# Two quarters of a split-precision feed-forward: high and low part of h in one pass of 512 columns, up and down chunks alternating

## The chip, the cores and the metric

The kernel runs on one core of a Trainium2 chip. The metric is the device time of one execution in microseconds.

## The reference

Two blocks run one after the other on 256 tokens of width 1024. The first has two layers, each with three kinds of attention and then a feed-forward; the second mixes attention, a Fourier, a convolution and a pooling branch and is untouched here. All is in float32. The feed-forward of the first block is

```
hdn = modulate(rmsnorm(x, norm2_g[l]), shift2, scale2)
ff = jnp.square(jax.nn.relu(hdn @ w_ff1[l])) @ w_ff2[l]
x = x + gate2[:, None, :] * ff
```

with `w_ff1` 1024 x 4096 and `w_ff2` 4096 x 1024.

## The kernel before

A float32 product is made of three products of rounded parts: each weight chunk is split into `w_hi` and `w_lo`, each activation into a high and a low part, and hi\*hi, hi\*lo and lo\*hi are added up in PSUM. A chunk is 8 x 128 rows by 256 columns of weights (1 MB). For each of the 8 row tiles and each of two halves of 128 output features, TensorE (PE) does three matmuls of 128x256 (lines 1758, 1760, 1762 in `products`), 48 in a chunk.

The program of a layer is a list of chunks, `j` = 0 to 74; the last 32, from `FF` = 43 on, are the feed-forward. I call `j - FF` the step, 0 to 31. The 4096 hidden features are in four quarters; `FF_ORDER` says that the steps are up 0, up 1, down 0, up 2, down 1, up 3, down 2, down 3, four chunks of each. An up chunk writes one of the two PSUM banks `dense` in turn; a down chunk adds to one of four banks `acc` (`first_s` twice, `first_t`, `first_o`).

Every engine walks the same list. Around step `j` each does, in this order:

- ScalarE (ACT): rounds the first half of chunk `j + 2` to `w_hi` (line 554; it waits until the PE has used the first half of chunk `j`), evacuates chunk `j`, rounds the second half of chunk `j + 2`. To evacuate an up chunk is ReLU (2140) and twice a square (2145, 2149).
- VectorE (DVE): makes `w_lo` of the first half of chunk `j + 2` by subtraction (560), makes the low part of the squared activation (2379), makes `w_lo` of the second half, and then does the *folds* of that step.

A fold belongs to other work: a 1 MB unit of a modulation matrix is multiplied by a column and added to the unit before (lines 588 and 592 in layer 0, 608 and 610, in two visits, in layer 1). The table `FOLDS` puts them at these steps of the feed-forward: in layer 0 one each at 2, 3 and 5, two at 7, one each at 8 to 26; in layer 1 one visit each at 3 to 10 and 13 to 20. When a group of folds is complete, the PE adds it up over the partitions in `group_sum` (line 245), placed in its queue at a fixed step. In layer 0 the sum at step 12 waits for the fold of step 10, that at 20 for the fold of step 18; in layer 1 the sum at step 12 waits for the fold of step 10, that at 22 for the fold of step 20. At step 4 of either layer another sum of the same line stands, over a unit that is not folded. `keep_group` (569, 574) moves such sums off on the DVE.

SyncE (SP) issues the loads in one queue: weight chunk `j` when the DVE has finished `w_lo` of chunk `j - 3`, and between them the fold units, each when an earlier fold is done.

```
for j in range(N_CHUNKS):
...
    split_ahead(partial(split_low, dve), base + j, 0)
...
    evacuate(j)
    split_ahead(partial(split_low, dve), base + j, 1)
...
    if j >= FF:
        for unit in folds_at(base + j):
            fold(dve, unit)
```

Of the kernel before, what the change touches and what calls it, by code (L numbers as in the profile page):

```python
# [51 lines left out]
GB, WSB, GC, WMB, GA, WMLA, WOUT, FF = 21, 25, 27, 31, 33, 37, 39, 43  # L52
FF_ORDER = [("up", 0), ("up", 1), ("down", 0), ("up", 2), ("down", 1), ("up", 3), ("down", 2), ("down", 3)]
FF_STEPS = [(kind, q, c) for kind, q in FF_ORDER for c in range(4)]
N_CHUNKS = FF + len(FF_STEPS)

# [81 lines left out]


def out_first(j):  # L140
    return WSB if j < GC else WMB if j < GA else WMLA
# [7 lines left out]
def units_of(j):  # L149

    if is_down(j):
        return 0
    if j == UKV:
        return 4
    return 2 if is_out(j) else 1

# [4 lines left out]
DONE = [sum(max(1, units_of(i % N_CHUNKS)) for i in range(g)) for g in range(DEPTH * N_CHUNKS + 1)]  # L161
UP_NO = {FF + i: 4 * q + c for i, (kind, q, c) in enumerate(FF_STEPS) if kind == "up"}
DOWN_END = {q: FF + i + 1 for i, (kind, q, c) in enumerate(FF_STEPS) if kind == "down" and c == 3}

# [11 lines left out]
def constants_first():  # L176
# [34 lines left out]
                    prob_ready=24, arg_ready=8, arg_exp=8, prob_t_ready=24, o_hi_made=12, o_ready=12,  # L211
                    gate_ready=12, merge_added=8, merged_hi=4, merged_ready=4, ff_hi_made=16, ff_ready=16,
                    x_ready=4)
# [64 lines left out]
def layers(nc, a, keep, out):  # L278
    with ExitStack() as stack:
# [1444 lines left out]
        def layer(l, next_x_ready, following=None):  # L1724
# [14 lines left out]
                Counted(first_sems[n], FIRST_COUNTS[n] * l) for n in ("gate_ready", "merge_added", "merged_hi", "merged_ready"))  # L1739
            ff_hi_made, ff_ready, x_ready = (Counted(first_sems[n], FIRST_COUNTS[n] * l) for n in ("ff_hi_made", "ff_ready", "x_ready"))  # L1740

# [4 lines left out]
            def tensor(pe):  # L1746
# [172 lines left out]
                def by_features(j, out, w, x, nk, width=P, **options):  # L1919
# [3 lines left out]
                    return products(j, outs, nk, **options)  # L1923

                def lead(j, chunks):

# [23 lines left out]
                def chunk(j):  # L1950
# [31 lines left out]
                    elif is_out(j):  # L1982
                        branch = {WSB: SB, WMB: MB, WMLA: MLA}[out_first(j)]
                        reach(pe, o_ready, 4 * branch + 4)
                        for e in range(2):
                            by_features(j, two(bank_of(u + e)), [part[:, :, CW * e:CW * e + CW] for part in w],
                                        (o_hi[branch], o_lo[branch]), 4, frees=e == 1).then_inc(unit_done, 1)
                    elif is_down(j):
                        _, q, c = FF_STEPS[j - FF]
# [46 lines left out]
            def scalar(act, link, logged):  # L2036
# [54 lines left out]
                def after_values(n):  # L2091
                    act.wait_ge(values_done[l], n + 1)
                    act.activation(o_hi[n // 4][:, n % 4, :], o_bank[:, 0:S], ACT.Copy).then_inc(o_hi_made.sem, 1)

                def evacuate(j):
                    if UQ <= j < UKV or is_out(j) or WOUT <= j < FF or is_down(j):
                        return
                    for e in range(units_of(j)):
# [39 lines left out]
                        else:  # L2138
                            n, (_, q, c) = UP_NO[j], FF_STEPS[j - FF]
                            act.activation(relu[n % 2], two, ACT.Relu).then_inc(done, 1)  # L2140
                            wait_evacuated(act, u)
                            if n >= 2:

                                reach(act, ff_ready, n - 1)
                            act.activation(relu_sq[n % 2], relu[n % 2], ACT.Square)
                            if c == 0 and q >= 2:

                                act.wait_ge(unit_done, DONE[base + DOWN_END[q - 2]])
                            act.activation(ff_hi[q % 2][:, 2 * c:2 * c + 2, :], relu[n % 2],
                                           ACT.Square).then_inc(ff_hi_made.sem, 1)  # L2150

# [85 lines left out]
            def vector(dve, link):  # L2237
# [111 lines left out]
                def evacuate_out(j, e):  # L2349
# [10 lines left out]
                    if first == 2:  # L2360
                        wait_evacuated(dve, u)
                        dve.tensor_tensor(merged[:, t:t + 2, :], merged[:, t:t + 2, :], gated[:, t:t + 2, :],
                                          ALU.add).then_inc(merge_added.sem, 1)

                def evacuate(j):
                    if QL <= j < CKV:
# [3 lines left out]
                    if j in ropes:  # L2370
                        rope(j)
                    elif WOUT <= j < FF:
                        u = RING[base + j]
                        dve.wait_ge(unit_done, DONE[base + j] + 1)
                        residual(2 * (j - WOUT), dense[u % 2], 16, j == FF - 1).then_inc(evacuated[u % 2], 1)
                    elif j in UP_NO:
                        n, (_, q, c) = UP_NO[j], FF_STEPS[j - FF]
                        reach(dve, ff_hi_made, n + 1)
                        dve.tensor_tensor(ff_lo[q % 2][:, 2 * c:2 * c + 2, :], relu_sq[n % 2],
                                          ff_hi[q % 2][:, 2 * c:2 * c + 2, :].bitcast(F32),  # L2380
                                          ALU.subtract).then_inc(ff_ready.sem, 1)
# [437 lines left out]
```

## Time and profile before

| | |
|---|---|
| time, median of 3 runs | 1375.18 us (1375.07 to 1375.34) |
| the profiled execution | 1374.65 us, its span 1372.5 us |
| PE busy in the span | 1329.8 us, 97% |
| DVE busy | 942.5 us, 69% |
| ACT busy | 737.4 us, 54% |
| feed-forward of layer 0, layer 1 | from 337 to 526 us, from 831 to about 1026 us |

The profiled execution lasted 2.15 us longer than its span, the part that lies around the recorded instructions. Matmuls overlap in the records: the distance from start to start says what one costs.

### The profile page before, as it was taken

How to read it: one execution, taken by the hardware profiler on the slowest of the kernel's cores; microseconds unless marked ns; L12 is line 12 of the kernel's file. 1: busy time of each engine (PE TensorE's matmuls, PEld its weight loads, DVE VectorE, ACT ScalarE, POOL GpSimd, SP SyncE). 2: the span in 40 equal slices, each digit the busy share in tenths (PEclk: the TensorE clock that was granted, in tenths of full speed). 3: DMA queues.
4: the chain of work that ended last, by engine and by line, in shares of the span. 5: the costliest groups of instructions: out<-in, count | busy, mean ns of one | idle time of the engine just before them, and what ended most of it. 6: DMA issues, size and time to landing. Idle time of an engine off the chain costs nothing.

```text
span 1372.5 us, 24612 instructions
## 1 busy us (share of the span) xinstructions
PE 1329.8 (97%) x10268; PEld 1218.2 (89%) x10268; DVE 942.5 (69%) x1367; ACT 737.4 (54%) x1203; POOL 60.5 (4%) x49
## 2 busy tenths in 40 slices
PE   6999999999999999999999999999999999998998
PEld 3998899998999998998999998999997778687987
DVE  3877976667688876478755566978575656538673
ACT  3565475564645534555666555544554555426562
POOL 0010000201000001010000210000100000011000
PEclk9999999999999999999999999999999999999999
DMA  9974555677799995744744467976552122132430
GB/s 345 356 237 166 168 209 180 211 255 240 234 323 374 357 372 181 228 132 132 275 154 128 150 218 261 318 244 220 177 167 92 62 93 81 43 101 73 144 123 31
DMA packets 194721, 269.51 MB, mean 196 GB/s; under 512 B 5037, under 2 KB 174386, under 8 KB 188338
## 3 DMA queue, kind: packets, MB, share of 16 engines
q1 hardware_dynamic: 194610, 267.94, 57.8%
q8 instruction: 81, 1.33, 0.4%
q14 instruction: 30, 0.25, 0.1%
HBM read 266.87 MB, written 1.05 MB: 195 GB/s over the span
## 4 chain that ended last, share of the span: by engine, by line
PE 78%; DVE 12%; ACT 5%; issue 3%; SPq 1%; DMA 1%; DVEq 0%; ACTq 0%
PE first_dense L1758 13%; PE first_dense L1762 12%; PE first_dense L1760 12%; PE first_dense L1075 5%; PE first_dense L1078 5%; PE first_dense L1077 5%; DVE first_w_lo L560 3%; PE first_s L1758 2%; PE first_s L1762 2%; PE first_s L1760 2%; PE first_dense L1937 2%; ACT first_w_hi L554 1%; PE first_o L1762 1%; PE first_t L1762 1%; PE first_t L1760 1%
## 5 line engine op out<-in xcount | busy, mean ns | idle before, releaser
L560 DVE TENSOR_TENSOR first_w_lo<-first_raw,first_w_hi 128x1024 fp32r<-128x1024 f32 (+2 forms) x304 | 366.5, 1219 | 185.0 <-ACT first_w_hi L554 182.9
L554 ACT ACTIVATE first_w_hi<-first_raw 128x1024 fp32r<-128x1024 f32 (+2 forms) x304 | 313.5, 1041 | 232.2 <-PE first_dense L1762 90.6
L1758 PE MATMUL first_dense<-first_h_parts,first_w_hi 128*128 128x256 f32 x1312 | 374.5, 285 | 3.0 <-DVE first_h_parts L2392 1.7
L1760 PE MATMUL first_dense<-first_h_parts,first_w_hi 128*128 128x256 f32 x1312 | 371.1, 283 | 0.0
L1762 PE MATMUL first_dense<-first_h_parts,first_w_lo 128*128 128x256 f32 x1312 | 371.0, 283 | 0.0
L1758 PEld LDWEIGHTS first_dense<-first_h_parts,first_w_hi 128*128 128x128 f32 x1312 | 251.5, 192 | 12.4 <-issue 8.1
L1760 PEld LDWEIGHTS first_dense<-first_h_parts,first_w_hi 128*128 128x128 f32 x1312 | 251.6, 192 | 0.0
L1762 PEld LDWEIGHTS first_dense<-first_h_parts,first_w_lo 128*128 128x128 f32 x1312 | 251.6, 192 | 0.0
L1077 PE MATMUL first_dense<-first_parts,first_w_hi 128*128 128x512 f32 (+1 forms) x400 | 137.0, 342 | 0.0
L1075 PE MATMUL first_dense<-first_h_parts,first_w_hi 128*128 128x512 f32 (+1 forms) x336 | 118.4, 352 | 1.4 <-DVE first_w_lo L731 0.9
L1078 PE MATMUL first_dense<-first_h_parts,first_w_lo 128*128 128x512 f32 (+1 forms) x336 | 115.6, 344 | 0.0
L731 DVE TENSOR_TENSOR first_w_lo<-first_raw,first_w_hi 128x1024 fp32r<-128x1024 f32 x56 | 68.1, 1224 | 48.2 <-ACT first_w_hi L724 47.8
L724 ACT ACTIVATE first_w_hi<-first_raw 128x1024 fp32r<-128x1024 f32 x56 | 58.9, 1055 | 48.7 <-PE first_dense L1078 48.6
L1077 PEld LDWEIGHTS first_dense<-first_parts,first_w_hi 128*128 128x128 f32 x400 | 75.8, 190 | 9.4 <-issue 1.0
L1758 PE MATMUL first_dense<-first_parts,first_w_hi 128*128 128x256 f32 x280 | 80.3, 287 | 0.7 <-DVE first_area L2291 0.7
L1760 PE MATMUL first_dense<-first_parts,first_w_hi 128*128 128x256 f32 x280 | 79.2, 283 | 0.0
L1762 PE MATMUL first_dense<-first_parts,first_w_lo 128*128 128x256 f32 x280 | 79.2, 283 | 0.0
L1075 PEld LDWEIGHTS first_dense<-first_h_parts,first_w_hi 128*128 128x128 f32 x336 | 63.6, 189 | 16.7 <-issue 8.7
L1758 PE MATMUL first_s<-first_parts,first_w_hi 128*128 128x256 f32 x256 | 72.8, 284 | 0.0
L1762 PE MATMUL first_s<-first_parts,first_w_lo 128*128 128x256 f32 x256 | 72.4, 283 | 0.0
L1760 PE MATMUL first_s<-first_parts,first_w_hi 128*128 128x256 f32 x256 | 72.4, 283 | 0.0
L1078 PEld LDWEIGHTS first_dense<-first_h_parts,first_w_lo 128*128 128x128 f32 x336 | 63.6, 189 | 7.7
(418 smaller groups left out, 2624.4 us busy)
## 6 DMA issues: line engine op xcount, KB each, us to landing
first_raw<-in_w_in SPq DMA_DIRECT2D x78, 1024.0 KB, 5.3
first_raw<-in_w_ff SPq DMA_DIRECT2D x64, 1024.0 KB, 7.9
first_units<-in_w_ada SPq DMA_DIRECT2D x34, 1024.0 KB, 6.6
first_units<-in_w_mod SPq DMA_DIRECT2D x17, 1024.0 KB, 6.8
first_raw<-in_w_out SPq DMA_DIRECT2D x16, 1024.0 KB, 5.3
first_mb<-in_w_ada SPq DMA_DIRECT2D x10, 1024.0 KB, 7.9
first_mb<-in_w_mod SPq DMA_DIRECT2D x7, 1024.0 KB, 7.3
first_raw<-in_w_uq SPq DMA_DIRECT2D x6, 768.0 KB, 4.4
```

The source lines that it names most:

```text
L554: act.activation(w_hi[g % SPLIT][:, c], raw[g % CHUNK_RING][:, c], ACT.Copy).then_inc(hi_made, 1)
L560: dve.tensor_tensor(w_lo[g % SPLIT][:, c], raw[g % CHUNK_RING][:, c], w_hi[g % SPLIT][:, c].bitcast(F32), ALU.subtract).then_inc(lo_made, 1)
L724: act.activation(in_tiles(w_hi[place2(l, c, SPLIT)][:])[:, r, :], in_tiles(raw[place2(l, c, CHUNK_RING)][:])[:, r, :], ACT.Copy).then_inc( ...
L731: engine.tensor_tensor(in_tiles(w_lo[place2(l, c, SPLIT)][:])[:, r, :], in_tiles(raw[place2(l, c, CHUNK_RING)][:])[:, r, :], hi.bitcast(F3 ...
L1075: pe.matmul(out, still[0](t), moving[0](t), start=t == i == 0, stop=False, skip_group_check=True)
L1077: pe.matmul(out, still[0](t), moving[1](t), start=False, stop=False, skip_group_check=True)
L1078: last = pe.matmul(out, still[1](t), moving[0](t), start=False, stop=t == KT - 1, skip_group_check=True)
L1758: pe.matmul(out, still[0](t), moving[0](t), start=start and t == n == 0, stop=False, skip_group_check=True)
L1760: pe.matmul(out, still[0](t), moving[1](t), start=False, stop=False, skip_group_check=True)
L1762: last = pe.matmul(out, still[1](t), moving[0](t), start=False, stop=stop and t == nk - 1, skip_group_check=True)
L1937: pe.matmul(at[i][:, c, :], part[:, t, c * P:(c + 1) * P], h_hi[:, t, :], start=part is w[i][0] and t == c == 0, stop=False, skip_group_ch ...
```

## The change

The up chunks of quarters 1 and 2 (`is_wide`, the second and third of four) take both `dense` banks. For each row tile and half of the features there is one matmul of `w_hi` against high and low part of h side by side, 512 columns (line 1941 of the new file), whose two halves land in the two halves of a bank, and one of `w_lo` against the high part, 256 columns (1943). ACT copies the right half of each bank out (`part_moved`), the DVE adds the left half to it, and then ACT does the ReLU and the two squares from SBUF as before. The low part of the square is made by the DVE at the next step, a down chunk. The order of the steps becomes up 0 (0 to 3), then up 1 and down 0 in turn (4 to 11), up 2 and down 1 in turn (12 to 19), and up 3, down 2, down 3 as before (20 to 31). The tables of folds and sums are unchanged, and so are their step numbers.

```
+FF_ORDER = [[("up", 0)], [("up", 1), ("down", 0)], [("up", 2), ("down", 1)], [("up", 3)], [("down", 2)], [("down", 3)]]
+FF_STEPS = [(kind, q, c) for kinds in FF_ORDER for c in range(4) for kind, q in kinds]
+def is_wide(j):
+    return j >= FF and FF_STEPS[j - FF][0:2] in (("up", 1), ("up", 2))
...
-    return 2 if is_out(j) else 1
+    return 2 if is_out(j) or is_wide(j) else 1
...
+                def wide_up(j):
+                    w = [view(part[(base + j) % SPLIT], j) for part in (w_hi, w_lo)]
+                    banks = [bank_of(RING[base + j] + c) for c in range(2)]
+                    for t in range(KT):
+                        if 2 * t in (0, KT):
+                            pe.wait_ge(lo_made, 2 * (base + j) + 1 + (t > 0))
+                        for c in range(2):
+                            f = slice(c * P, (c + 1) * P)
+                            pe.matmul(two(banks[c]), w[0][:, t, f], h_parts[:, :, t, :], start=t == 0, stop=False,
+                                      skip_group_check=True)
+                            last = pe.matmul(banks[c][:, 0:S], w[1][:, t, f], h_hi[:, t, :], start=False,
+                                             stop=t == KT - 1, skip_group_check=True)
+                            if t == KT - 1:
+                                last.then_inc(unit_done, 1)
+                        if 2 * t + 2 == KT:
+                            last.then_inc(half_used, 1)
...
# ACT
+                    if is_wide(j):
+                        r, u = relu[UP_NO[j] % 2], RING[base + j]
+                        for e in range(2):
+                            act.wait_ge(unit_done, DONE[base + j] + e + 1)
+                            act.activation(r[:, e, :], dense[(u + e) % 2][:, S:2 * S], ACT.Copy).then_inc(part_moved.sem, 1)
+                        for e in range(2):
+                            wait_evacuated(act, u + e)
+                        link(act.activation(r, r, ACT.Relu))
+                        up_squares(j)
+                        return
...
# DVE
+                    elif is_wide(j):
+                        r, u = relu[UP_NO[j] % 2], RING[base + j]
+                        for e in range(2):
+                            reach(dve, part_moved, 2 * WIDE_NO[j] + e + 1)
+                            dve.tensor_tensor(r[:, e, :], r[:, e, :], dense[(u + e) % 2][:, 0:S],
+                                              ALU.add).then_inc(evacuated[(u + e) % 2], 1)
                     elif j in UP_NO:
+                        up_low(j)
+                    elif is_down(j) and is_wide(j - 1):
+                        up_low(j - 1)
```

On the DVE, layer 0, steps 14 and 15 before (both up 2): for each, `w_lo` of the first half, the low part of the square, `w_lo` of the second half, a fold.

```order
L560 TENSOR_TENSOR first_w_lo<-first_raw,first_w_hi 128x1024 [waits first_hi_made]
L2379 TENSOR_TENSOR first_parts<-first_gate,first_parts 128x512 [waits first_ff_hi_made]
L560 TENSOR_TENSOR first_w_lo<-first_raw,first_w_hi 128x1024 [waits first_hi_made]
L592 SCALAR_TENSOR_TENSOR first_units<-first_units,first_small 128x2048 [waits first_unit_folded,first_raw_in3]
L560 TENSOR_TENSOR first_w_lo<-first_raw,first_w_hi 128x1024 [waits first_hi_made]
L2379 TENSOR_TENSOR first_parts<-first_gate,first_parts 128x512 [waits first_ff_hi_made]
L560 TENSOR_TENSOR first_w_lo<-first_raw,first_w_hi 128x1024 [waits first_hi_made]
L592 SCALAR_TENSOR_TENSOR first_mb<-first_mb,first_small,first_units 128x2048 [waits first_unit_folded,first_raw_in5]
```

The same two steps after the change (an up chunk of quarter 2, then a down chunk of quarter 1).

```order
L566 TENSOR_TENSOR first_w_lo<-first_raw,first_w_hi 128x1024 [waits first_hi_made]
L2428 TENSOR_TENSOR first_gate<-first_gate,first_dense 128x256 [waits first_part_moved] x2
L566 TENSOR_TENSOR first_w_lo<-first_raw,first_w_hi 128x1024 [waits first_hi_made]
L598 SCALAR_TENSOR_TENSOR first_units<-first_units,first_small 128x2048 [waits first_unit_folded,first_raw_in3]
L566 TENSOR_TENSOR first_w_lo<-first_raw,first_w_hi 128x1024 [waits first_hi_made]
L2409 TENSOR_TENSOR first_parts<-first_gate,first_parts 128x512 [waits first_ff_hi_made]
L566 TENSOR_TENSOR first_w_lo<-first_raw,first_w_hi 128x1024 [waits first_hi_made]
L598 SCALAR_TENSOR_TENSOR first_mb<-first_mb,first_small,first_units 128x2048 [waits first_unit_folded,first_raw_in5]
```

Two additions stand now between the two subtractions of the up step, and the low part has gone to the step behind; every fold has kept its place behind the second subtraction.

On ACT, an up step before:

```order
L554 ACTIVATE first_w_hi<-first_raw 128x1024 [waits first_half_used,first_raw_in2]
L2140 ACTIVATE first_gate<-first_dense 128x512 [waits first_unit_done]
L2145 ACTIVATE first_gate<-first_gate 128x512 [waits first_ff_ready,first_evacuated0]
L2149 ACTIVATE first_parts<-first_gate 128x512
L554 ACTIVATE first_w_hi<-first_raw 128x1024 [waits first_unit_done,first_raw_in2]
```

and an up step of quarter 1 after:

```order
L560 ACTIVATE first_w_hi<-first_raw 128x1024 [waits first_half_used,first_raw_in1]
L2140 ACTIVATE first_gate<-first_dense 128x256 [waits first_unit_done] x2
L2143 ACTIVATE first_gate<-first_gate 128x512 [waits first_evacuated1,first_evacuated0]
L2127 ACTIVATE first_gate<-first_gate 128x512 [waits first_ff_ready,first_act_link]
L2130 ACTIVATE first_parts<-first_gate 128x512
L560 ACTIVATE first_w_hi<-first_raw 128x1024 [waits first_unit_done,first_raw_in1]
```

The ReLU now stands behind a wait for the DVE's two additions, and the second rounding still stands behind the ReLU and the squares.

On the PE, the sum at step 12 of layer 0 before, between a down chunk and an up chunk:

```order
L1762 MATMUL first_o<-first_parts,first_w_lo0 128x256
L245 MATMUL first_misc<-first_units,keep_consts 32x512 [waits first_ssq_used,first_group_kept,first_unit_folded]
L245 MATMUL first_misc<-first_units,keep_consts 32x512 x3
L1758 MATMUL first_dense0<-first_h_parts,first_w_hi1 128x256 [waits first_lo_made,first_evacuated0]
L1760 MATMUL first_dense0<-first_h_parts,first_w_hi1 128x256
```

and after:

```order
L1769 MATMUL first_o<-first_parts,first_w_lo0 128x256
L251 MATMUL first_misc<-first_units,keep_consts 32x512 [waits first_ssq_used,first_group_kept,first_unit_folded]
L251 MATMUL first_misc<-first_units,keep_consts 32x512 x3
L1941 MATMUL first_dense0<-first_h_parts,first_w_hi1 128x512 [waits first_lo_made,first_evacuated1,first_evacuated0]
L1943 MATMUL first_dense0<-first_h_parts,first_w_lo1 128x256
```

The sum with its wait for the folds has kept its place; the up chunk behind it waits for both banks.

## Rows read from the trace of the kernel before

**Rows 1.** The page: busy time, share of the span and instructions of each engine.

```profile
PE 1329.8 (97%) x10268; PEld 1218.2 (89%) x10268; DVE 942.5 (69%) x1367; ACT 737.4 (54%) x1203; POOL 60.5 (4%) x49
```

**Rows 2.** Windows: stretch and length, busy time by engine, clock, DMA share, GB/s.

```profile
408.40:454.50 46.10, 46.10 (x388) 46.10 (x384) 39.72 (x31) 23.97 (x29) 0.00 (x0) 1.00 1.05 375
855.70:901.70 46.00, 46.00 (x387) 46.00 (x384) 41.25 (x40) 24.06 (x30) 0.00 (x0) 1.00 0.93 319
```

**Rows 3.** Timeline of the PE, layer 0, step 12: start, us, engine, line, tiles, count.

```profile
407.18 0.28 PE L1762 MATMUL first_o<-first_parts,first_w_lo 128*128 128x256 f32 x1
407.39 1.06 PE L245 MATMUL first_misc<-first_units,keep_consts 128*32 128x512 f32 x8
408.39 0.38 PE L1758 MATMUL first_dense<-first_h_parts,first_w_hi 128*128 128x256 f32 x1
```

**Rows 4.** Timeline of the PE: matmuls of 512 columns and 256 columns.

```profile
1100.08 0.39 PE L1075 MATMUL first_dense<-first_h_parts,first_w_hi 128*128 128x512 f32 x1
1100.31 0.39 PE L1077 MATMUL first_dense<-first_parts,first_w_hi 128*128 128x512 f32 x1
...
407.06 0.28 PE L1760 MATMUL first_o<-first_parts,first_w_hi 128*128 128x256 f32 x1
```

**Rows 5.** Timeline of the PE: the other three sums of groups of folds.

```profile
454.65 1.06 PE L245 MATMUL first_misc<-first_mb,keep_consts 128*32 128x512 f32 x8
...
901.93 1.07 PE L245 MATMUL first_misc<-first_pair_sums,first_choose 128*32 128x256 f32 x16
...
961.62 1.07 PE L245 MATMUL first_misc<-first_pair_sums,first_choose 128*32 128x256 f32 x16 [0.84 <-DVE first_pair_sums L610]
```

**Rows 6.** Timeline of the DVE, layer 0, steps 4 and 5, 10, and 14.

```profile
366.40 1.22 DVE L560 TENSOR_TENSOR first_w_lo<-first_raw,first_w_hi 128x1024 fp32r<-128x1024 f32 x1
...
371.09 0.44 DVE L569 STREAM_TRANSPOSE first_small<-first_misc 128x256 f32<-128x256 f32 x1
...
371.73 1.22 DVE L560 TENSOR_TENSOR first_w_lo<-first_raw,first_w_hi 128x1024 fp32r<-128x1024 f32 x1
...
404.98 2.35 DVE L592 SCALAR_TENSOR_TENSOR first_units<-first_units,first_small,first_mb 128x2048 f32<-128x2048 f32 x1
...
428.11 0.68 DVE L2379 TENSOR_TENSOR first_parts<-first_gate,first_parts 128x512 fp32r<-128x512 f32 x1
428.73 1.23 DVE L560 TENSOR_TENSOR first_w_lo<-first_raw,first_w_hi 128x1024 fp32r<-128x1024 f32 x1
429.87 2.35 DVE L592 SCALAR_TENSOR_TENSOR first_units<-first_units,first_small 128x2048 f32<-128x2048 f32 x1
432.13 1.22 DVE L560 TENSOR_TENSOR first_w_lo<-first_raw,first_w_hi 128x1024 fp32r<-128x1024 f32 x1
...
434.48 1.23 DVE L560 TENSOR_TENSOR first_w_lo<-first_raw,first_w_hi 128x1024 fp32r<-128x1024 f32 x1 [0.26 <-ACT first_w_hi L554]
```

**Rows 7.** Timeline of ACT: the ReLU of step 15 and the rounding behind it.

```profile
431.72 0.60 ACT L2140 ACTIVATE first_gate<-first_dense 128x512 f32<-128x512 f32 x1 [0.50 <-PE first_dense L1762]
...
433.41 1.04 ACT L554 ACTIVATE first_w_hi<-first_raw 128x1024 fp32r<-128x1024 f32 x1
```

**Rows 8.** Groups by line and form: count, busy us, mean ns of one.

```profile
L2346 DVE TENSOR_TENSOR first_parts<-first_o,first_parts 128x256 fp32r<-128x256 f32 x24 | 10.0, 417 | 0.1
...
L2111 ACT ACTIVATE first_area<-first_dense 128x256 f32<-128x256 f32 x2 | 0.7, 362 | 0.0
```

**Rows 9.** Timeline of the DVE, layer 1, at step 4 and at step 20.

```profile
860.78 1.22 DVE L560 TENSOR_TENSOR first_w_lo<-first_raw,first_w_hi 128x1024 fp32r<-128x1024 f32 x1
...
958.97 2.60 DVE L610 SCALAR_TENSOR_TENSOR first_pair_sums<-first_mb,first_small,first_pair_sums 128x1024 f32<-128x1024 f32 x2
```

**Rows 10.** Windows in the second block, columns as in rows 2.

```profile
1242.80:1245.70 2.90, 0.00 (x0) 0.00 (x0) 2.76 (x7) 1.47 (x4) 0.00 (x0) 1.00 0.68 200
...
1246.90:1250.10 3.20, 3.20 (x17) 3.20 (x17) 3.06 (x9) 1.50 (x4) 0.00 (x0) 0.50 0.07 18
```

**Rows 11.** DMA queue from 408 to 503 us (share of 16 engines); ACT's waits.

```profile
q1 hardware_dynamic: 19945, 34.76, 102.9%
...
ACT first_w_hi L554 <- DMA first_raw<-in_w_ff: 43.6, 17, 4.5
```

More of the change, by code:

```diff
@@ L52 @@
 GB, WSB, GC, WMB, GA, WMLA, WOUT, FF = 21, 25, 27, 31, 33, 37, 39, 43
-FF_ORDER = [("up", 0), ("up", 1), ("down", 0), ("up", 2), ("down", 1), ("up", 3), ("down", 2), ("down", 3)]
-FF_STEPS = [(kind, q, c) for kind, q in FF_ORDER for c in range(4)]
+FF_ORDER = [[("up", 0)], [("up", 1), ("down", 0)], [("up", 2), ("down", 1)], [("up", 3)], [("down", 2)], [("down", 3)]]
+FF_STEPS = [(kind, q, c) for kinds in FF_ORDER for c in range(4) for kind, q in kinds]
 N_CHUNKS = FF + len(FF_STEPS)
@@ L162 @@
 UP_NO = {FF + i: 4 * q + c for i, (kind, q, c) in enumerate(FF_STEPS) if kind == "up"}
+WIDE_NO = {j: n for n, j in enumerate(j for j in UP_NO if is_wide(j))}
 DOWN_END = {q: FF + i + 1 for i, (kind, q, c) in enumerate(FF_STEPS) if kind == "down" and c == 3}
@@ L211 @@
                     prob_ready=24, arg_ready=8, arg_exp=8, prob_t_ready=24, o_hi_made=12, o_ready=12,
-                    gate_ready=12, merge_added=8, merged_hi=4, merged_ready=4, ff_hi_made=16, ff_ready=16,
+                    gate_ready=12, merge_added=8, merged_hi=4, merged_ready=4, ff_hi_made=16, ff_ready=16, part_moved=2 * len(WIDE_NO),
                     x_ready=4)
@@ L1739, in layer @@
                 Counted(first_sems[n], FIRST_COUNTS[n] * l) for n in ("gate_ready", "merge_added", "merged_hi", "merged_ready"))
-            ff_hi_made, ff_ready, x_ready = (Counted(first_sems[n], FIRST_COUNTS[n] * l) for n in ("ff_hi_made", "ff_ready", "x_ready"))
+            ff_hi_made, ff_ready, part_moved, x_ready = (Counted(first_sems[n], FIRST_COUNTS[n] * l)
+                                                for n in ("ff_hi_made", "ff_ready", "part_moved", "x_ready"))
             def norm_added(norm):
@@ L1987, in chunk @@
                                         (o_hi[branch], o_lo[branch]), 4, frees=e == 1).then_inc(unit_done, 1)
+                    elif is_wide(j):
+                        wide_up(j)
                     elif is_down(j):
@@ L2093, in after_values, with up_squares @@
                     act.activation(o_hi[n // 4][:, n % 4, :], o_bank[:, 0:S], ACT.Copy).then_inc(o_hi_made.sem, 1)
+                def up_squares(j):
+                    n, (_, q, c) = UP_NO[j], FF_STEPS[j - FF]
+                    if n >= 2:
+                        reach(act, ff_ready, n - 1)
+                    act.activation(relu_sq[n % 2], relu[n % 2], ACT.Square)
+                    if c == 0 and q >= 2:
+                        act.wait_ge(unit_done, DONE[base + DOWN_END[q - 2]])
+                    act.activation(ff_hi[q % 2][:, 2 * c:2 * c + 2, :], relu[n % 2],
+                                   ACT.Square).then_inc(ff_hi_made.sem, 1)
                 def evacuate(j):
                     if UQ <= j < UKV or is_out(j) or WOUT <= j < FF or is_down(j):
+                        return
[8 more added lines that the diff above has]
+                        up_squares(j)
                         return
@@ L2138, in evacuate @@
                         else:
-                            n, (_, q, c) = UP_NO[j], FF_STEPS[j - FF]
+                            n = UP_NO[j]
                             act.activation(relu[n % 2], two, ACT.Relu).then_inc(done, 1)
                             wait_evacuated(act, u)
[L2142 to L2150, printed above, removed]
+                            up_squares(j)
                 if l:
@@ L2363, in evacuate_out, with up_low @@
                                           ALU.add).then_inc(merge_added.sem, 1)
+                def up_low(j):
+                    n, (_, q, c) = UP_NO[j], FF_STEPS[j - FF]
+                    reach(dve, ff_hi_made, n + 1)
+                    dve.tensor_tensor(ff_lo[q % 2][:, 2 * c:2 * c + 2, :], relu_sq[n % 2],
+                                      ff_hi[q % 2][:, 2 * c:2 * c + 2, :].bitcast(F32),
+                                      ALU.subtract).then_inc(ff_ready.sem, 1)
                 def evacuate(j):
@@ L2375, in evacuate @@
                         residual(2 * (j - WOUT), dense[u % 2], 16, j == FF - 1).then_inc(evacuated[u % 2], 1)
-                    elif j in UP_NO:
[L2377 to L2381, printed above, removed]
+                    elif is_wide(j):
+                        r, u = relu[UP_NO[j] % 2], RING[base + j]
[3 more added lines that the diff above has]
+                                              ALU.add).then_inc(evacuated[(u + e) % 2], 1)
+                    elif j in UP_NO:
+                        up_low(j)
+                    elif is_down(j) and is_wide(j - 1):
+                        up_low(j - 1)
                     elif is_down(j) and FF_STEPS[j - FF][1] == 3:
```

## The prediction

> **What bounds the kernel now.** I read the page's busy times first: the PE is busy for 97% of the span [rows 1]. Then the windows of the stretches that the change touches: from 408.4 to 454.5 us and from 855.7 to 901.7 us the PE is busy all the time at full clock, but the DVE already for 39.7 of 46.1 us and 41.3 of 46.0 us, and in layer 0 the DMA engines are full too [rows 2]. So matmul time is what a change can win here, and the vector engine is what it can run into: it has 6.4 and 4.7 us free in eight steps. The timeline at step 12 says how thin this is. The fold that the sum at step 12 needs runs from 404.98 to 407.33 us [rows 6], the sum starts at 407.39 [rows 3], just when the PE would have come to it anyway (a matmul started at 407.18 us). In layer 1 the sum at step 22 is late already: 0.84 us of idle PE, ended by the fold [rows 5]. The folds have no slack.
>
> **What the change takes away.** Matmuls of 256 columns start 0.12 us apart (407.06, 407.18) [rows 3, 4], those of 512 columns 0.23 us apart (1100.08, 1100.31; 0.227 over a run of them) [rows 4]. A row tile and half cost 3 x 0.120 = 0.360 us and will cost 0.227 + 0.120 = 0.347 us. With 16 of them in a chunk the chunk goes from 5.76 to 5.55 us, and 16 such chunks in both layers (8 each) save 256 x 0.013 = 3.4 us. That is 0.25% and the whole gain on offer.
>
> The Trainium skill (TensorE: Matmul & The Clock Gate, section "Back-to-back issue gap") gives for a lone matmul columns / 2.4 + 2.5 ns, which would be 109 and 216 ns, so less fixed cost for each matmul than the trace has and a gain of 256 x 2.5 ns = 0.6 us instead of 3.4; the trace disagrees at both sizes (120 and 227 ns), and I go by the trace.
>
> **What it adds on the other engines.** For an up step of quarter 1 or 2: two copies from PSUM on ACT, 0.36 us each by the nearest group, which reads the same bank [rows 8]; two additions with one operand in PSUM on the DVE, 0.42 us each by line 2346, which has the same shape [rows 8] (bounds: 0.36 us, the copy of as many columns, and 0.68 us, the low part of twice as many [rows 6]). What matters more is where the additions stand. Before, nothing on ACT's path to the second rounding waited for the DVE. Now the DVE adds, ACT then does ReLU, two squares and the rounding, and the DVE's next instruction in its queue is the subtraction that needs this rounding. From the start of the ReLU to the start of that subtraction the trace has 431.72 to 434.48 = 2.76 us [rows 6, 7]. The fold that could fill this time stands behind the subtraction, so the DVE idles.
>
> **The DVE's time for a pair of steps.** Start to start: a subtraction takes 1.14 us (428.73 to 429.87), a low part 0.62 (428.11 to 428.73), a fold 2.26 (429.87 to 432.13) [rows 6].
> - Up step: 1.14 + 0.33 (first addition to the second, overlapping 0.09 as other neighbours do) + 0.42 (second) + 0.04 (handing over) + 2.76 + 1.14 = 5.83 us, with a fold 8.09.
> - Down step: 0.62 + 2 x 1.14 = 2.90 us, with a fold 5.16.
>
> Together 13.25 us against 5.55 + 5.76 = 11.31 us on the PE. The DVE becomes the bound of these steps and falls behind by 1.94 us in each pair that has two folds. The PE feels it at the sums, which wait for the last fold of their group (and by some 1 us stalls on `w_lo` before, which only bring part of the same wait forward).
>
> **The four stretches, laid end to end on the DVE.**
> - Layer 0, to the sum at step 12. The first subtraction of step 4 starts at 366.40 us [rows 6] and nothing ahead of it changes. Steps 4 to 10 have folds 0, 1, 0, 2, 1, 1, 1 and one removal of a sum, 0.64 us (371.09 to 371.73) [rows 6]: 5.83 + 5.80 + 5.83 + 7.42 + 8.09 + 5.16 + 8.09 = 46.1 us, so 412.5 us instead of 407.39: **+5.1**.
> - Layer 0, from that sum (S) to the one at step 20. The PE starts the up chunk at S + 1.00 [rows 3], is through at S + 6.71; second copy, second addition, ReLU chain: the second subtraction of step 12 starts at S + 10.37, its fold ends the step at S + 13.8. Steps 13 to 18: 5.80 + 3 x 8.09 + 2 x 5.16 = 40.4 us. Together 54.2 us; before it was 407.39 to 454.65 = 47.26 [rows 3, 5]: **+6.9**.
> - Layer 1, to step 12. Here a visit takes 2.6 us (958.97, two of 1.3) [rows 9] and there is one in each of steps 4 to 10: 4 x 8.43 + 3 x 5.50 + 0.64 = 50.9 us from 860.78 [rows 9], so 911.6 instead of 901.93 [rows 5]: **+9.7**.
> - Layer 1, from there to step 22: S + 11.5 after the subtraction of step 12, then steps 13 to 20 (four down or narrow, counting step 20, plus three wide with a visit, and step 13 with its removal): 6.14 + 3 x 8.43 + 4 x 5.50 = 53.4; together 64.9 against 59.69 [rows 5]: **+5.2**.
>
> The sum is 26.9 us. The 3.4 us saved on the PE are in it and worth nothing: within a stretch the PE only arrives at the sum earlier.
>
> Not in this sum are the loads. Weights of chunk `j + 3` are asked for when the DVE has done chunk `j`, and fold units when an older fold is done, all in one queue of SP; ACT waited 43.6 us for weights before [rows 11], and the queue kept the DMA engines at 103% of their share [rows 11]. A later DVE makes SP ask later, but a longer stretch also gives the DMA more time for the same bytes: 54.2 instead of 47.3 us leaves it some 13% free. I take 1.5 us, with 0 and 10 us (a quarter of those waits no longer covered) as ends.
>
> **The clock.** The stalls before the sums are single idle times of the PE of some 4 to 7 us. The trace has one that fills the window from 1242.8 to 1245.7 us; behind it the granted clock was 0.50 for at least 3.2 us [rows 10], the lower of the two levels, 1.2 GHz, with the PE busy throughout, so 1.6 us were lost. The 0.84 us of idle PE at step 22 cost nothing of the kind (the windows of the feed-forward are at 1.00). Four stalls at 1.6 us are 6.4 us, with 0 and 11 as ends. They add up, because what follows a sum hangs on the PE's first chunk.
>
> The Trainium skill (the same page, section "HAM oscillation") says that idle gaps between bursts of matmuls put the engine back to the lower clock, each time anew; the trace agrees with its one gap of 2.9 us.
>
> **The sum:** 26.9 + 1.5 + 6.4 = 34.8 us on the profiled execution's 1374.65 us gives 1409.4; that execution stands 0.5 us under the median of the runs, so I predict **1410 us**.
>
> **Rivals.**
> - *The clock holds* (for it: only one gap in the trace tells; against: all four stalls are longer than its 2.9 us). 1375.2 + 28.4 = 1403.6 us. Chance 0.14.
> - *The loads run late* (for it: rows 11, and both kinds of unit in one queue, so a chunk waits behind a fold unit that waits for the DVE; against: the longer stretches). 10 us and a longer fold stretch: 1375.2 + 26.9 + 10 + 6.4 = 1418.5, up to 1425 us. Chance 0.13.
> - *The DVE's new wait is covered* and the kernel gets faster. It needs the pair to fit in 11.31 us, that is, the 2.8 us idle between addition and subtraction shrunk to 0.9 or less, and the fold of step 10 no later than before. It would be so if ACT could round ahead of the ReLU; the order of its queue speaks against it. Then 1375.2 - 3.4 = 1371.8 us. Chance 0.04.
> - *No change*: the wider matmuls bring less than 3 us and the folds just fit. 1374 to 1377 us. Chance 0.03, since even a DVE without any lag would end the fold of step 10 some 7.5 us after the PE is through with that step (copies 0.76, additions and handing over 0.50, then 2.76, 1.14 and 2.35), and the sum is due after 5.76.
> - *Milder of the same*, additions of 0.36 us, folds partly caught up: 1393 to 1403 us. Chance 0.08.
>
> The forecast keeps 0.58. The range of 8 in 10 takes in the case without the clock and the nearer half of the late loads: 1398 to 1422 us. A measurement here tells about 0.2% (2.8 us) from no change. Faster 0.04, same 0.03, slower 0.93.
>
> **What would show it.** In the trace after: matmuls of line 1941 followed by the next 0.227 us later, and wide chunks of 5.55 us; idle DVE of 2.8 us between line 2428 and line 566 in each of 16 up steps, released by ACT's rounding; four waits of the PE before line 251, of 4 to 7 us, ended by the folds (lines 598 and 616), at about 412 and 467 us in layer 0; behind each a stretch with the clock at 0.50; nothing new from step 23 on. The prediction is wrong if the PE does not wait at line 251, or if ACT's longest waits are for `in_w_ff`.

## The result: 1412.4 us, slower by 2.65%

The changed kernel takes 1412.44 us (median of 4 runs, 1411.13 to 1413.49), the kernel before 1375.26 us beside it (1375.07 to 1375.36). The ratio on record is 1.0265, with a 95% interval of 1.0252 to 1.0278; the two medians above divide to 1.0270, a difference that matters nowhere below. The profiled execution's span is 1410.8 us, 38.3 us more than before.

### The profile page after: what moved, and what is told of

It reads as the page before. It is cut to its first block, busy times and chain, and to the rows that moved or that the text cites. A ratio compares the mean times of both kernels' runs of the same rounds, so it can differ in the third digit from the quotient of the medians.

```text
span 1410.8 us, 24180 instructions
## 1 busy us (share of the span) xinstructions
PE 1338.1 (95%) x10012; PEld 1206.9 (86%) x10012; DVE 950.8 (67%) x1399; ACT 746.4 (53%) x1235; POOL 60.5 (4%) x49
## 4 chain that ended last, share of the span: by engine, by line
PE 65%; DVE 20%; ACT 7%; issue 4%; DMA 2%; SPq 1%; ACTq 0%; DVEq 0%
PE first_dense L1765 10%; PE first_dense L1767 10%; PE first_dense L1769 10%; DVE first_w_lo L566 6%; PE first_dense L1081 5%; PE first_dense L1084 5%; PE first_dense L1083 5%; DVE first_pair_sums L616 2%; ACT first_w_hi L560 2%; PE first_dense L1962 2%; DMA first_raw<-in_w_ada 1%; PE first_misc L251 1%; PE first_s L1765 1%; DVE first_units L598 1%; PE first_s L1769 1%
## 5 line engine op out<-in xcount | busy, mean ns | idle before, releaser
L1765 PE MATMUL first_dense<-first_h_parts,first_w_hi 128*128 128x256 f32 x1056 | 303.6, 287 | 5.3 <-DVE first_w_lo L566 3.5
L1767 PE MATMUL first_dense<-first_h_parts,first_w_hi 128*128 128x256 f32 x1056 | 300.1, 284 | 0.0
L1765 PEld LDWEIGHTS first_dense<-first_h_parts,first_w_hi 128*128 128x128 f32 x1056 | 203.9, 193 | 14.3 <-issue 8.5
L1767 PEld LDWEIGHTS first_dense<-first_h_parts,first_w_hi 128*128 128x128 f32 x1056 | 204.1, 193 | 0.0
L1769 PEld LDWEIGHTS first_dense<-first_h_parts,first_w_lo 128*128 128x128 f32 x1056 | 203.9, 193 | 0.0
L1941 PE MATMUL first_dense<-first_h_parts,first_w_hi 128*128 128x512 f32 x256 | 93.2, 405 | 2.2 <-DVE first_w_lo L566 2.1
L1081 PEld LDWEIGHTS first_dense<-first_h_parts,first_w_hi 128*128 128x128 f32 x336 | 63.6, 189 | 16.7 <-issue 8.7
L1765 PE MATMUL first_s<-first_parts,first_w_hi 128*128 128x256 f32 x256 | 72.8, 284 | 0.0
```

Of the source, the lines that this page charges most:

```text
L1081: pe.matmul(out, still[0](t), moving[0](t), start=t == i == 0, stop=False, skip_group_check=True)
L1765: pe.matmul(out, still[0](t), moving[0](t), start=start and t == n == 0, stop=False, skip_group_check=True)
L1767: pe.matmul(out, still[0](t), moving[1](t), start=False, stop=False, skip_group_check=True)
L1769: last = pe.matmul(out, still[1](t), moving[0](t), start=False, stop=stop and t == nk - 1, skip_group_check=True)
L1941: pe.matmul(two(banks[c]), w[0][:, t, f], h_parts[:, :, t, :], start=t == 0, stop=False, skip_group_check=True)
```

## The profile after

The page's busy times, to be held against [rows 1], and its chain of work that ended last, by engine:

```profile
PE 1338.1 (95%) x10012; PEld 1206.9 (86%) x10012; DVE 950.8 (67%) x1399; ACT 746.4 (53%) x1235; POOL 60.5 (4%) x49
...
PE 65%; DVE 20%; ACT 7%; issue 4%; DMA 2%; SPq 1%; ACTq 0%; DVEq 0%
```

No engine has much more work than before, and still the share of the DVE on the chain is 20%, where it was 12% before (and the PE's 78% fell to 65%). So time went to waiting for the DVE, not to the DVE's work. The waits of the whole execution, of the engine named first for the one behind the arrow (us in total, times, longest):

```profile
PE first_misc L251 <- DVE first_pair_sums L616: 10.4, 2, 6.7
...
DVE first_w_lo L566 <- ACT first_w_hi L560: 225.0, 133, 6.0
...
ACT first_gate L2143 <- DVE first_gate L2428: 48.2, 16, 6.5
ACT first_w_hi L560 <- DMA first_raw<-in_w_ff: 22.2, 9, 4.2
```

ACT's waits for weights, 43.6 us before [rows 11], are down to 22.2: the loads are not what is late. New is ACT's wait of the ReLU for the additions, 16 times, once in each wide step. The four sums that the PE was to wait for, in the timeline of the PE (start, us, ..., idle before it and what ended it), with the matmuls behind the first:

```profile
414.37 1.08 PE L251 MATMUL first_misc<-first_units,keep_consts 128*32 128x512 f32 x4 [6.09 <-DVE first_units L598]
...
416.24 0.80 PE L1941 MATMUL first_dense<-first_h_parts,first_w_hi 128*128 128x512 f32 x1
417.05 0.63 PE L1941 MATMUL first_dense<-first_h_parts,first_w_hi 128*128 128x512 f32 x1
...
419.33 0.40 PE L1941 MATMUL first_dense<-first_h_parts,first_w_hi 128*128 128x512 f32 x1
...
471.39 1.08 PE L251 MATMUL first_misc<-first_mb,keep_consts 128*32 128x512 f32 x4 [6.10 <-DVE first_mb L598]
...
930.92 1.08 PE L251 MATMUL first_misc<-first_pair_sums,first_choose 128*32 128x256 f32 x8 [6.72 <-DVE first_pair_sums L616]
...
997.13 1.50 PE L251 MATMUL first_misc<-first_pair_sums,first_choose 128*32 128x256 f32 x10 [3.69 <-DVE first_pair_sums L616]
```

These answer to [rows 3, 5], where the longest wait was 0.84 us: the PE now sits idle for 6.09, 6.10, 6.72 and 3.69 us, each time until a fold is done. Behind the first one a matmul of 512 columns takes 0.63 us at 417.05, and 0.40 us at 419.33. The windows from each of these sums on show why (columns as in [rows 2]: stretch and length, busy time by engine, clock, DMA share, GB/s):

```profile
414.37:419.00 4.63, 4.63 (x17) 2.58 (x18) 4.01 (x4) 0.00 (x0) 0.00 (x0) 0.50 0.78 263
471.40:477.00 5.60, 5.60 (x25) 3.94 (x26) 4.00 (x4) 0.00 (x0) 0.00 (x0) 0.50 0.85 275
930.90:934.40 3.50, 3.48 (x21) 2.02 (x22) 2.96 (x3) 0.00 (x0) 0.00 (x0) 0.50 0.64 204
997.10:1002.60 5.50, 5.47 (x33) 4.20 (x34) 2.96 (x3) 0.00 (x0) 0.00 (x0) 0.50 0.58 197
```

The granted clock is 0.50, the lower level of 1.2 GHz, while the PE works all but without a break. The DVE at steps 14 and 15 shows where its time goes, beside [rows 6]:

```profile
436.46 1.22 DVE L566 TENSOR_TENSOR first_w_lo<-first_raw,first_w_hi 128x1024 fp32r<-128x1024 f32 x1
437.59 0.74 DVE L2428 TENSOR_TENSOR first_gate<-first_gate,first_dense 128x256 f32<-128x256 f32 x2
441.23 1.22 DVE L566 TENSOR_TENSOR first_w_lo<-first_raw,first_w_hi 128x1024 fp32r<-128x1024 f32 x1 [2.89 <-ACT first_w_hi L560]
442.37 2.34 DVE L598 SCALAR_TENSOR_TENSOR first_units<-first_units,first_small 128x2048 f32<-128x2048 f32 x1
444.63 1.22 DVE L566 TENSOR_TENSOR first_w_lo<-first_raw,first_w_hi 128x1024 fp32r<-128x1024 f32 x1
```

After the two additions the DVE does nothing for 2.89 us, until ACT's second rounding is there, although the fold that follows needs nothing from it. The same idle time, 2.88 to 2.90 us, stands in each of the 16 wide steps. The step takes 444.63 - 436.46 = 8.17 us. ACT in the same step:

```profile
438.43 0.63 ACT L2143 ACTIVATE first_gate<-first_gate 128x512 f32<-128x512 f32 x1 [3.29 <-DVE first_gate L2428]
439.09 0.63 ACT L2127 ACTIVATE first_gate<-first_gate 128x512 f32<-128x512 f32 x1
439.63 0.61 ACT L2130 ACTIVATE first_parts<-first_gate 128x512 fp32r<-128x512 f32 x1
440.15 2.94 ACT L560 ACTIVATE first_w_hi<-first_raw 128x1024 fp32r<-128x1024 f32 x3
```

So each engine waits for the other in turn: ReLU behind the additions, rounding behind ReLU and squares, subtraction behind the rounding, fold behind the subtraction.

**How the kernels are compared.** I lay the starts of the four sums beside each other, in distances (us). "L0 12" is the distance from the sum at step 4 of layer 0 to that at step 12, and so on; the last column goes from the sum at step 22 of layer 1 to the end of the span. All are differences of starts in the timelines of the PE, good to 0.01 us. The distance L0 28 holds no wide chunk. The stretch from the sum at step 28 of layer 0 to that at step 4 of layer 1 is not in the table; it takes 352.8 us before and after.

| kernel | step 4, L0 | L0 12 | L0 20 | L0 28 | L1 12 | L1 22 | to the end |
|---|---|---|---|---|---|---|---|
| before | 360.13 | 47.26 | 47.26 | 47.26 | 47.26 | 59.69 | 410.9 |
| after | 361.13 | 53.24 | 57.02 | 49.76 | 56.99 | 66.21 | 413.7 |
| round_first | 361.80 | 47.16 | 46.67 | 47.27 | 46.63 | 59.07 | 411.3 |
| fold_first | 361.39 | 47.21 | 46.73 | 47.26 | 46.64 | 59.07 | 411.2 |
| both | 362.36 | 46.64 | 46.62 | 47.26 | 46.63 | 59.07 | 411.3 |
| order_only | 360.88 | 47.92 | 47.92 | 47.26 | 48.17 | 59.70 | 410.9 |
| busy_wait | 363.03 | 53.65 | 54.99 | 47.26 | 57.01 | 64.65 | 411.3 |
| wide_only | 360.55 | 56.12 | 56.69 | 47.26 | 57.82 | 66.20 | 411.3 |
| small_folds_old | 361.45 | 47.26 | 47.26 | 47.26 | 47.26 | 58.78 | 410.9 |
| small_folds_new | 361.35 | 46.63 | 46.63 | 47.26 | 47.51 | 58.26 | 411.3 |

## The experiments

Theory: the additions have put ACT's second rounding behind the DVE, the DVE idles 2.9 us ahead of its second subtraction, and with a fold in each step it sets the pace; the PE pays at the sums, and once more by the clock. Rivals: the PE loses time in the wide chunk itself (two banks, `w_lo`), the alternation of the steps costs, or the loads are late. Each timed kernel ran beside the kernel before (1376.0 us in both groups of runs).

**round_first: ACT rounds early.** The second half of chunk `j + 2` is rounded behind the copies and ahead of the ReLU.

```
 # ACT, in a wide step, behind the two copies
+    split_ahead(partial(split_high, act), base + j, 1)
     for e in range(2):
         wait_evacuated(act, u + e)
...
-    split_ahead(partial(split_high, act), base + j, 1)
+    if not is_wide(j):
+        split_ahead(partial(split_high, act), base + j, 1)
```

> The changed kernel with one thing moved: in a wide step ACT rounds the second half of the next chunk but one right after its two copies, ahead of the ReLU that waits for the vector engine. Theory (the vector engine's 2.8 us idle behind its additions makes it the bound of the pair of steps): that wait shrinks to some 0.4 us, the pair fits in 11.31 us of matmuls, the long waits of the PE before the sums go (under 1 us each) and with them the low clock; time about 1372 us, 0.2% under the kernel before. Rival 1 (the loads, or the 512-column matmuls themselves, cost the time): still 1400 us or more. Rival 2 (the additional instructions of ACT and the vector engine are too many wherever they stand): 1385 to 1400 us.

Measured: 1373.98 us, ratio 0.9985 (0.9976 to 0.9994). The DVE at the same two steps:

```profile
429.16 0.74 DVE L2430 TENSOR_TENSOR first_gate<-first_gate,first_dense 128x256 f32<-128x256 f32 x2
429.82 1.22 DVE L566 TENSOR_TENSOR first_w_lo<-first_raw,first_w_hi 128x1024 fp32r<-128x1024 f32 x1
430.96 2.34 DVE L598 SCALAR_TENSOR_TENSOR first_units<-first_units,first_small 128x2048 f32<-128x2048 f32 x1
```

The 2.89 us are gone, and with them the long waits of the PE: 0.46 us is left at step 12 of layer 0, and the 0.84 us at step 22 of layer 1 that were there before the change. One rounding in each wide step, moved ahead in ACT's queue, brings 38 us back.

**fold_first: the DVE folds early.** The folds of a wide step (and the visits of layer 1 in the same way, not shown) stand behind the additions, ahead of the second subtraction; ACT is as in the changed kernel.

```
 # DVE, behind evacuate(j)
+    if is_wide(j):
+        for unit in folds_at(base + j):
+            fold(dve, unit)
...
     split_ahead(partial(split_low, dve), base + j, 1)
...
-    if j >= FF:
+    if j >= FF and not is_wide(j):
```

> The changed kernel with the other side of the same wait filled: in a wide step the vector engine does its fold before the second subtraction, while ACT does ReLU, squares and rounding; nothing moves on ACT. Theory: 2.3 us of fold fill the 2.8 us of wait, a pair takes 13.25 - 2.26 = 11.0 us, long waits before the sums go; about 1373 us (1371 to 1376), with perhaps one stall of 1 us where two folds stand in one step. Rival (ACT's own queue or the loads are the bound): 1390 us or more.

Measured: 1373.99 us, ratio 0.9985 (0.9976 to 0.9994).

```profile
439.44 0.74 DVE L2428 TENSOR_TENSOR first_gate<-first_gate,first_dense 128x256 f32<-128x256 f32 x2
440.10 2.34 DVE L598 SCALAR_TENSOR_TENSOR first_units<-first_units,first_small,first_mb 128x2048 f32<-128x2048 f32 x1
443.07 2.36 DVE L566 TENSOR_TENSOR first_w_lo<-first_raw,first_w_hi 128x1024 fp32r<-128x1024 f32 x2 [0.63 <-ACT first_w_hi L560]
```

ACT's chain is as long as before, but the fold now fills the time (0.63 us idle). So the length of the chain alone costs nothing; what cost was that work which could run stood behind it.

**both: the two together.**

> ACT rounds the second half early AND the DVE folds early. If either already takes the DVE's idle time away, both together bring nothing more: 1371 to 1374.5 us, within 0.2% of either one alone, no wait of the PE over 1 us before line 251. If what is left of the 3.4 us is lost in folds that are still a little late, it would come to 1371 to 1372 us, 2 us below either one alone.

Measured: 1372.93 us, ratio 0.9981 (0.9972 to 0.9990), the fastest version; its interval overlaps those of the two alone. The table shows what is won: each distance with four wide chunks is 0.63 us shorter than before.

**order_only: the alternation alone.** `is_wide` returns False, so all up chunks are as before, in the new order.

> Only the new order of the chunks (up and down in turn), with the up chunks as before: three matmuls of 256 columns, one ReLU from PSUM. Theory: the order costs nothing or nearly so, at most a bank and a fold met slightly later; 1375 to 1378 us. Rival (it is the order that makes folds or activations late): 1385 us or more.

Measured: 1377.56 us, ratio 1.0010 (1.0001 to 1.0018). Three distances are 0.7 to 0.9 us longer, nearly all of it waits of the PE for a fold at the sum that ends each (0.59, 0.59 and 0.84 us), and that is all the order costs.

**wide_only: the wide chunks alone**, in the old order of steps; the low part of the square is made one step later.

```
-FF_ORDER = [[("up", 0)], [("up", 1), ("down", 0)], [("up", 2), ("down", 1)], ...
+FF_ORDER = [[("up", 0)], [("up", 1)], [("down", 0)], [("up", 2)], [("down", 1)], ...
...
+                        if is_wide(j - 1):
+                            up_low(j - 1)
```

> The wide up chunks in the old order of steps (up 1 four times, then down 0, and so on), so the other half of the change by itself. If the long chain from addition to subtraction is the cause, it does not need the alternation: the up steps stand back to back, each 8.1 us on the DVE with a fold against 5.6 us on the PE, both dense banks are held until the additions are done, and the PE loses some 32 us in the two layers, in waits of 1 to 4 us for the banks (before line 1941) rather than in four long ones before line 251, so with hardly any lower clock: 1400 to 1412 us. If it were the alternation together with the wide chunks (down chunks whose low part is made a step later) that costs, the old order would be near the kernel before, 1372 to 1380 us.

Measured: 1411.91 us, ratio 1.0261 (1.0247 to 1.0275), as slow as the whole change. Its waits of the PE:

```profile
PE first_dense L1941 <- DVE first_gate L2430: 23.4, 12, 3.8
...
PE first_misc L251 <- DVE first_pair_sums L616: 3.0, 2, 2.2
...
PE first_misc L251 <- DVE first_units L598: 1.6, 1, 1.6
PE first_misc L251 <- DVE first_mb L598: 0.7, 1, 0.7
```

The last two rows come from the same view of layer 0 alone, and one wait before line 1941 with the window behind it is:

```profile
384.74 0.77 PE L1941 MATMUL first_dense<-first_h_parts,first_w_hi 128*128 128x512 f32 x1 [2.99 <-DVE first_gate L2430]
...
384.70:388.20 3.50, 3.46 (x12) 2.98 (x12) 0.68 (x1) 2.73 (x4) 0.00 (x0) 0.55 1.02 395
```

The same idle DVE (2.89 us in each wide step) is paid here before the next wide chunk, for the banks, since wide steps stand back to back. The distances grow by 8.9, 9.4, 10.6 and 6.5 us, 35.4 in all. The waits for the banks and at line 251 come to 28.7 us, of which the 0.84 us at step 22 of layer 1 were there before. Hardly any low clock was expected here, and that was a miss. Within or behind each of the four longest waits for the banks (2.99, 3.83, 3.47 and 2.74 us) the clock fell as well, in the first for the 3.5 us above and in the others as these windows show:

```profile
435.70:438.90 3.20, 3.20 (x12) 2.71 (x11) 1.19 (x2) 1.98 (x3) 0.00 (x0) 0.50 1.00 341
889.70:895.90 6.20, 5.11 (x16) 4.37 (x17) 3.32 (x5) 2.73 (x4) 0.00 (x0) 0.50 1.05 392
954.10:957.60 3.50, 2.69 (x8) 2.34 (x9) 0.70 (x3) 2.67 (x4) 0.00 (x0) 0.55 0.20 66
```

With half of the PE's busy time in these four windows lost (3.46 + 3.20 + 5.11 + 2.69 = 14.5 us), my estimate is some 7 us for the clock; what makes the small rest was not taken apart. Where the idle time is paid depends on the order; that it is paid does not.

**busy_wait: the PE works while it waits.** Ahead of the four sums stand 25, 25, 28 and 14 matmuls of 512 columns into the PSUM tile that the sum overwrites; they change no output. The wait until that tile is free (`free_rows`) has moved ahead of them.

```
+    free_rows(group)
+    for _ in range({(1, "ada", 0): 25, (1, "ada", 1): 25, (1, "mod2", 1): 28, (1, "mod2", 2): 14}.get(group, 0)):
+        pe.matmul(rows_ps[:], h_hi[:, 0, 0:P], h_parts[:, :, 0, :], start=True, stop=True, ...)
     pe.wait_ge(unit_folded, FOLDED.index(unit) + 1)
-    free_rows(group)
```

> The changed kernel with extra matmuls of 512 columns, their results thrown away, ahead of the four sums for which the PE waits (25, 25, 28 and 14 of them, 0.22 us each, a little less than the idle time), so that the PE is busy while the vector engine is late. Theory of the clock: the waits stay, but the granted clock stays at full speed behind them, and about 9 us come back: 1402 to 1406 us. Rival (the low clock behind the stalls costs nothing, since the vector engine is the bound anyway): 1411 to 1414 us.

Measured: 1405.06 us, ratio 1.0210 (1.0196 to 1.0224). The windows around the first of the four sums and around the third (they start at 416.68 and 928.70 us here), about the times at which the clock was low after the change, and below them wider ones around the second and the fourth (471.67 and 993.35 us):

```profile
412.00:418.90 6.90, 6.50 (x34) 4.44 (x34) 5.76 (x5) 3.00 (x4) 0.00 (x0) 1.00 0.78 248
926.00:933.00 7.00, 6.64 (x46) 4.90 (x45) 5.57 (x6) 0.87 (x2) 0.00 (x0) 1.00 0.45 145
...
466.00:480.00 14.00, 13.60 (x93) 11.51 (x92) 8.78 (x7) 6.30 (x9) 0.00 (x0) 1.00 0.91 308
988.00:1004.00 16.00, 15.51 (x124) 14.02 (x124) 10.97 (x11) 7.13 (x10) 0.00 (x0) 1.00 0.52 171
```

The PE is busy nearly throughout and the clock stays at 1.00, and the four distances behind the sums shrink by 57.02 - 54.99, 49.76 - 47.26, 66.21 - 64.65 and 413.7 - 411.3, together 8.5 us. The two distances that start at step 4, where no long wait lies ahead, do not shrink (53.24 and 53.65; 56.99 and 57.01): the wait for the folds stays. That profile also has 2 us more at the program's start. By the medians, which come from two groups of runs, the clock is worth 1412.44 - 1405.06 = 7.4 us; about 9 us were expected.

**small_folds_new and small_folds_old: less to fold.** The changed kernel and the kernel before, with the folds of layer 1's modulation and all later ones done over 32 columns only; most of those sums are left out.

```
+    part = 32 if unit[0] == 1 else SLOT
...
-    done = dve.tensor_scalar(w[:], w[:], factor, None, ALU.mult)
+    done = dve.tensor_scalar(w[:, 0:part], w[:, 0:part], factor, None, ALU.mult)
```

> The changed kernel with the folds of layer 1's modulation and of the second block's done over 32 columns only; most of these sums are left out. The DVE then has room for its 2.8 us of idling. Theory (the DVE as bound through folds): no wait over 1 us before line 251, clock at 1.00, and the 3.4 us of the wider matmuls come out: 1370.5 to 1373.5 us. Rival (the up step itself loses time on the PE, through the wait for two banks or w_lo): still over 1380 us.

> The kernel before with the same folds cut to 32 columns, the partner of the run ahead of it. The folds are hidden in the kernel before but for 0.8 us, so 1373.5 to 1375.5 us; the changed kernel with small folds is to be 2.5 to 3.5 us below this one. If the wider matmuls bring nothing, the two are the same within 1 us.

Measured: 1373.54 and 1374.75 us (ratios 0.9981, 0.9972 to 0.9990, and 0.9990, 0.9981 to 0.9999). With room on the DVE the whole change costs nothing, so the wide chunk itself loses nothing on the PE (the first time is at the very end of the range that was expected, 1370.5 to 1373.5 us). But the pair differs by 1.2 us, not by the 2.5 to 3.5 expected. By the table the wide chunks save 4 x 0.63 = 2.5 us, of which 0.81 us is given back at one sum and 0.4 us behind the last sum:

```profile
902.14 1.07 PE L251 MATMUL first_misc<-first_pair_sums,first_choose 128*32 128x256 f32 x16 [0.81 <-DVE first_pair_sums L617]
```

The fold ahead of this sum is small and still late, because copies, additions, ReLU, squares, rounding and subtraction run one behind the other before it: the DVE idles for 2.89 us there too, from 897.52 to 900.41 us.

## Why the prediction was right

The forecast was 1410 us by four stalls at line 251; the measured time is 1412.4, and each step of its main line is in the trace. Several sizes were off, and one term stands for something that was not there; they are named below.

- **The DVE's wait.** Forecast 2.8 us of idle DVE in a wide step, measured 2.89; forecast 8.09 us for an up step with a fold and 5.16 for a down step, measured 8.17 and 5.14 (the down step ahead, from 431.32 to 436.46 us). round_first and fold_first take the wait away from one side each, and the slowdown goes: shown. The Trainium skill (PSUM — Partial Sum Buffer, section "Engine vs sequencer instructions") says that the queues of ACT and DVE are strictly first in, first out; the 2.89 us of idle DVE ahead of a fold that was ready agree with it.
- **The four stretches.** Forecast +5.1, +6.9, +9.7, +5.2 us. Measured without the clock: 53.24 - 47.26 = +6.0; 57.02 - 47.26 = 9.8, less 2.0 for the clock by busy_wait, +7.7; 56.99 - 47.26 = +9.7; 66.21 - 59.69 = 6.5, less 1.6, +5.0. Together 28.4 us, against 26.9. The excess sits in layer 0, and the DVE's timeline shows it. In the first stretch (0.9 us): each of the four wide steps is 0.08 us longer than forecast; step 7, where two folds stand side by side, takes 7.59 us and not 7.42 (from 385.17 to 392.76); step 5 takes 5.29 instead of 5.16; the seven terms of the forecast add up to 46.22 us and not to 46.1; and the end of the last fold with the hand-over to the PE, 0.14 us, was left out. In the second (0.8 us), read in busy_wait where the clock is full: the second subtraction of step 12 starts 10.68 us behind the sum instead of 10.37, the removal of the sum takes 0.85 us instead of 0.64, and the rest is again the 0.08 us of the three wide steps and the end of the last fold.
- **The loads.** I had 1.5 us for them, and 26.9 + 1.5 is just the 28.4 measured. But the term is not confirmed by that: the DVE waited for no load in these stretches, and ACT's waits for weights fell. No run shows the 1.5 us; that they stand in the sum just where the DVE's time came out 1.5 us too short is luck.
- **The clock.** The mechanism was right, the size was not: forecast 4 x 1.6 = 6.4 us, measured 8.5 by the distances (7.4 by the medians). The term of 1.6 came from a stretch of 3.2 us at 0.50; behind these stalls the PE worked 3.5 to 5.6 us at 0.50. The rival in which the clock holds (1403.6 us) is what busy_wait built, and it took 1405.1. One of the four stalls is 3.69 us long and so a little shorter than the 4 to 7 us announced. The Trainium skill (TensorE: Matmul & The Clock Gate, section "HAM oscillation — how this bites in real kernels") has the clock fall anew at every idle gap of this kind; four stalls and four low stretches agree, and so does their absence in busy_wait.
- **The gain.** This price was wrong: 0.013 us for a row tile and half, 3.4 us in all. Within the wide chunks of `both` the matmul behind one of 512 columns starts 0.235 us later on average, not 0.227 as in the stretch of 512-column matmuls that I had read at 1100 us, and a wide chunk takes 5.56 to 5.76 us instead of 5.55; the sums stand 0.63 us earlier per four chunks, 2.5 us in all. It changed next to nothing in the sum, where the gain was worth nothing.
- **The rest.** The step 4 sum of the profiled execution stood 1.0 us later than before, and 0.4 us came behind the last sum, where nothing new was forecast; every version with wide chunks has them (411.2 to 411.3 against 410.9 in the table), and what makes them was not looked for. The first belongs to the start of the program, not to the change: over all ten profiles that sum stands anywhere from 360.13 to 363.03 us, with no relation to the edits.

The sum of the parts is 28.4 + 8.5 + 1.0 + 0.4 = 38.3 us, the difference of the spans. It comes out by construction, since the distances make up the span; the causes rest on the experiments.

Of the rivals, the covered wait ("if ACT could round ahead of the ReLU", 1371.8 us) is what round_first made of it, at 1374.0 us, 2.0 us under the kernel before beside it where 3.4 were forecast.

## What to carry to other kernels

When a helper engine gets one more hand-over in the middle of its step, look at what stands behind its next wait in the queue: independent work behind a wait for a partner's long chain is lost time, and putting either that work ahead of the wait or the partner's product ahead of its chain gives all of it back. Price a stall of the PE with the slow clock behind it, since here each stall of 3.7 to 6.7 us cost 1.6 to 2.5 us more (the distances of busy_wait). And a gain of 0.2% on the bounding engine can only be collected if nothing on the others gets later, so the order of all queues has to be changed together with the matmuls.

## What was not expected of the hardware

- Behind stalls of 6.1, 6.1 and 3.7 us the PE worked at a granted clock of 0.50 for 4.6, 5.6 and 5.5 us, and behind the longest one, 6.7 us, for only 3.5. The clock had fallen during the stall already, at 412.2 us in the first, so part of the low time lay in the stall itself (two windows, ahead of the fall and behind it, with the PE idle in both):

```profile
408.30:412.10 3.80, 0.00 (x0) 0.00 (x0) 1.27 (x2) 3.77 (x6) 0.00 (x0) 1.00 1.00 375
412.20:414.30 2.10, 0.00 (x0) 0.00 (x0) 2.10 (x2) 0.49 (x1) 0.00 (x0) 0.50 0.72 240
```

  The cost of a stall did not grow with its length: by the distances of busy_wait it was 1.6 us behind the longest and 2.4 behind the shortest.
- The pitch behind a matmul of 512 columns is not one number: 0.227 us over a run of them before, 0.235 us on average (0.231 to 0.243 as the mean of one chunk) where matmuls of 512 and 256 columns alternate, and in the wide chunks the matmul behind one of 256 columns starts 0.117 us later on average instead of 0.120.
- The program's start (up to the sum at step 4 of layer 0) moved by up to 2.9 us over the ten profiled executions, more than the gain in question, so that effects of 1 us are to be read from distances inside the trace.
